# Moving the split weights' SBUF tensors 64 bytes down in a two-layer decoder trunk

## The reference

```python
h = rmsnorm(x, g_mix[0]);  x = x + gla_group(h, ...) @ w_out[0]
h = rmsnorm(x, g_ffn[0]);  x = x + (silu(h @ w_dense_gate) * (h @ w_dense_up)) @ w_dense_down
kv = rmsnorm(x, g_kv) @ w_kv                       # shared keys and values
h = rmsnorm(x, g_mix[1]);  x = x + diff_group(h, kv, ...) @ w_out[1]
h = rmsnorm(x, g_ffn[1]);  x = x + moe_swiglu(h, w_router, w_gate, w_up, w_down)   # top 2 of 8
out = rmsnorm(x, g_final)
```

## Time and profile before

| | us |
|---|---|
| median of 2 runs | 1590.91 |
| lowest and highest | 1589.26, 1592.56 |
| profiled execution | 1586.55 |
| its span, first to last instruction | 1584.8 |
| TensorE busy | 1499.1 (95% of the span) |
| VectorE busy | 1144.9 (72%) |
| ScalarE busy | 957.8 (60%) |

### The profile page before, as it was taken

The page is one execution under the profiler, slowest core; times in us unless marked ns, Lnnn a source line. Parts: engine busy times, 40 slices in busy tenths (PEclk is TensorE's granted clock), DMA queues, the critical chain, the costliest instruction groups (busy, mean ns, idle before and its releaser), DMA issues.

```text
span 1584.8 us, 19889 instructions
## 1 busy us (share of the span) xinstructions
PE 1499.1 (95%) x7534; PEld 1252.8 (79%) x7534; DVE 1144.9 (72%) x941; ACT 957.8 (60%) x868; POOL 7.9 (1%) x18
## 2 busy tenths in 40 slices
PE   4997899998978789999999999999999999999996
PEld 4995689998865668888887887887888888888885
DVE  3453454545557479879879878988887987987984
ACT  4553244334445377766767677767767677766773
POOL 1000000000000000000000000000000000000000
PEclk8995799999985899999999999999999999999998
DMA  9561154565512159989989999998997998998990
GB/s 295 184 206 53 54 169 164 187 209 185 165 54 80 53 195 384 387 298 375 387 319 347 385 334 335 384 376 287 394 376 288 384 380 289 385 385 285 380 384 29
DMA packets 201923, 428.34 MB, mean 270 GB/s; under 512 B 8848, under 2 KB 42672, under 8 KB 201872
## 3 DMA queue, kind: packets, MB, share of 16 engines
q1 hardware_dynamic: 200736, 424.18, 74.2%
q0 software_dynamic: 1136, 3.47, 0.9%
HBM read 426.57 MB, written 1.05 MB: 270 GB/s over the span
## 4 chain that ended last, share of the span: by engine, by line
PE 91%; DVE 5%; ACT 2%; DMA 1%; issue 1%; SPq 0%; DVEq 0%; ACTq 0%
PE ps L1130 27%; PE ps L1132 27%; PE ps L1131 27%; PE ps L1448 2%; PE ps L1426 2%; PE ps L1469 2%; DVE w_lo L682 1%; PE ps L1274 1%; DMA raw<-in_w_mem_kv_dram 1%; PE ps L1156 1%; PE ps L1249 1%; ACT w_hi L395 0%; PE ps L1327 0%; DVE small L739 0%; ACT sc L431 0%
## 5 line engine op out<-in xcount | busy, mean ns | idle before, releaser
L1063 DVE TENSOR_TENSOR e_wlo<-raw,e_whi 128x2048 fp32r<-128x2048 f32 x336 | 750.7, 2285 | 113.6 <-ACT e_whi L618 113.4
L618 ACT ACTIVATE e_whi<-raw 128x2048 fp32r<-128x2048 f32 x336 | 620.7, 1915 | 43.5 <-PE ps L1132 43.5
L1130 PE MATMUL ps<-e_whi,act_hi 128*128 128x512 f32 x1344 | 534.4, 398 | 2.9 <-DVE act_lo L1030 1.5
L1132 PE MATMUL ps<-e_wlo,act_hi 128*128 128x512 f32 x1344 | 523.9, 390 | 0.0
L1131 PE MATMUL ps<-e_whi,act_lo 128*128 128x512 f32 x1344 | 523.2, 389 | 0.0
L1130 PEld LDWEIGHTS ps<-e_whi,act_hi 128*128 128x128 f32 x1344 | 252.4, 188 | 57.5 <-issue 5.3
L1131 PEld LDWEIGHTS ps<-e_whi,act_lo 128*128 128x128 f32 x1344 | 252.6, 188 | 54.5 <-issue 3.8
L1132 PEld LDWEIGHTS ps<-e_wlo,act_hi 128*128 128x128 f32 x1344 | 252.3, 188 | 53.5
L682 DVE TENSOR_TENSOR w_lo<-raw,w_hi 128x2048 fp32r<-128x2048 f32 (+2 forms) x68 | 148.4, 2198 | 159.3 <-ACT w_hi L395 159.2
L395 ACT ACTIVATE w_hi<-raw 128x2048 fp32r<-128x2048 f32 (+2 forms) x68 | 124.1, 1839 | 105.7 <-PE ps L1132 89.7
L623 ACT ACTIVATE act_hi<-ps 128x512 fp32r<-128x512 f32 x56 | 33.5, 598 | 199.0 <-PE ps L1469 199.0
(11 more groups left out here) (200 smaller groups left out, 1116.9 us busy)
## 6 DMA issues: line engine op xcount, KB each, us to landing
raw<-in_w_exp_gate_dram SPq DMA_DIRECT2D x112, 1024.0 KB, 7.0
raw<-in_w_exp_up_dram SPq DMA_DIRECT2D x112, 1024.0 KB, 7.2
raw<-in_w_exp_down_dram SPq DMA_DIRECT2D x112, 1024.0 KB, 7.5
raw<-in_w_dense_gate_dram SPq DMA_DIRECT2D x11, 1024.0 KB, 5.2
raw<-in_w_dense_up_dram SPq DMA_DIRECT2D x11, 1024.0 KB, 5.4
raw<-in_w_dense_down_dram SPq DMA_DIRECT2D x11, 1024.0 KB, 5.7
raw<-in_w_out_dram SPq DMA_DIRECT2D x8, 1024.0 KB, 5.0
raw<-in_w_in_a_dram SPq DMA_DIRECT2D x7, 1024.0 KB, 6.6
```

Source lines behind the costliest of these rows:

```text
L618: nc.scalar.activation(e_whi[:, (s - NPRE) % E_SPLIT, :], raw[:, s % RAW, :], ACT.Copy)\
L1063: nc.vector.tensor_tensor(e_wlo[:, r, :], raw[:, s % RAW, :], e_whi[:, r, :].bitcast(F32), ALU.subtract).then_inc(lo_ready, 1)
L1130: nc.tensor.matmul(dst, l_hi, r_hi, start=start, stop=False)
L1132: return nc.tensor.matmul(dst, l_hi, r_lo, start=False, stop=stop)
```

## The change

The second padding becomes 264 numbers (1056 bytes), 64 bytes shorter:

```diff
-        sb("split_pad", [P, 280])
+        sb("split_pad", [P, 264])
```

## The result

| | before | after |
|---|---|---|
| median, us | 1590.91 (2 runs) | 1605.30 (2 runs: 1603.80, 1606.81) |
| profiled execution, us | 1586.55 | 1606.81 |
| its span, us | 1584.8 | 1605.0 |
| ratio, after to before | | 1.0106, 95% interval 1.0060 to 1.0152 |

The change makes the kernel about 1% slower, 9.5 to 24 us by the interval. The two spans differ by 20.2 us. A ratio of 1.0106 is inside what I called "within 2%", and the time is inside the range, but it is a real slowing and I had forecast none.

The account below looks back on a forecast made before the run. TensorE was taken as the bound, matmul count times distance; every term was 0, so 1586.55 + 0 = 1586.6 us profiled, 1590.9 as median (own range 1585 to 1600). The range that reached the rivals was 1550 to 1672.

Parts of the forecast that it names:

- within 2%: Whole kernel: the measured time lies within 2% of the time before, chance 0.55; slower 0.37, faster 0.08.
- What bounds the kernel: TensorE, never idle in an expert (125.00 of 125.00 us): time is the number of matmuls times what one costs.
- The count: Matmuls with an operand whose start moves: 5016 with weights moving, 1440 with weights stationary, together 6456.
- The step that failed: Price of a moving operand's new start: taken as 0 from 16-column operands at a 64-byte offset; ends 35 us faster, 920 slower.
- The term for stationary operands: Matmuls with weights stationary: 0 for the same reason as moving operands, up to 1440 x 4.2 = 6 us.
- The reading that the 13 ns are a wait for operands: Each matmul at full clock takes 13 ns beyond columns over clock, read as the array waiting for its operands.
- The bounds: Distance of matmuls in an expert: 219.7 ns if reads miss each other, 240 ns with one more piece per read.
- Rival 1: Moving reads fetched in 128-byte pieces need one more, 13.3 ns each: 67 us, 1658 us; chance 0.21, dearer form 0.13.
- Rival 2: Moving operands pay the 4.2 ns by phase seen for stationary ones: 21 us, 1612 us; chance 0.12.
- Rival 3: TensorE's moving and stationary reads, set 64 bytes apart, miss each other: wait falls to 6.3 ns, 1556 us; chance 0.11.
- Splits and their cover: VectorE and ScalarE splits: 0 change from 2285 and 1915 ns; each may grow 0.44 us before VectorE becomes the bound.
- The page rule: SBUF lines of 16 bytes: 64 bytes are four whole lines, accesses keep their place, so the sum is 0.

Follow-up runs that it names:

- w_only: The change for the stages before the experts alone, a 16-number padding putting the experts' tensors back; 1584.70 us, ratio 0.9980 to the kernel before the change.
- both_down: Split activations and split weights both 64 bytes lower than in the kernel before the change; 1588.33 us against 1588.67, ratio 0.9999.
- w128: The change with 128 bytes in place of 64, against the kernel before the change; ratio 1.0146, an expert 127.76 us.

## Why the prediction was right and wrong

- **What bounds the kernel** held. The effect in the experts is one distance times its count, TensorE stayed the bound, and nothing hid it: the experts' 24.1 us came through in full.
- **The count** held, but I multiplied it by a single price. By rows, 512-column matmuls with `act_hi` or `act_lo` stationary pay 6.6 ns (4560 of them; 6.0 as the mean over an expert), 256-column ones with 128 stationary columns gain 2 to 6 ns (1392 of them), those with 96 stationary columns 0.3 on the mean (117.9 to 117.6: one half of a slot loses nearly what the other gains), and the 264 of the dense down product pay nothing, as both their operands moved together.
- **The step that failed** is "Between ends so far apart the nearest row is the 64-byte offset that costs nothing ... I take 0". Those loads are 16 columns wide and 256 columns move over them, and their case says nothing of 512 columns moving over 128: such matmuls measured 6.6 ns with the same offset. The term for stationary operands, 0 "for the same reason", failed with it: they gained 2 to 6 ns. The sum should have been about +24 us in the experts and between -1.5 (by the distances) and -3 (by the medians of `w_only`) ahead of them.
- **The reading that the 13 ns are a wait for operands** fits all runs: at an unchanged 2.4 GHz (granted clock 1.00) the distance moved with the layout alone. That the wait is on the reading side was argued from it and is now likely; which of the reads waits is not shown.
- **The bounds** held: 233.3 is between 219.7 and 240. The range held the time, and was wide because I had no row between them; the forecast's own range, 1585 to 1600, did not hold it.
- **Rival 1** (one more piece per moving read) is refuted: 240 ns did not come, `both_down` has every moving read off its boundary for nothing, and 128 bytes, on the boundary, cost the same as 64.
- **Rival 2** (4.2 ns by phase, 1612 us) came nearest in microseconds, by accident: it charged the operand's own position, and `both_down` says that this costs nothing. What the earlier trace rows show is the same kind of effect, the position of the two reads to each other, as the halves that change places in `w128` show.
- **Rival 3** had the mechanism, the two reads' position to each other, with the wrong sign. I thought that both tensors at the same phase must be the bad place; for 512 columns it is the best of all that were tried, and only 256 columns over 128 stationary ones gained as this rival would have it. My argument against it ("with odd k the two are already 64 bytes apart and nothing changes") was the same mistake as the failed step.
- **Splits and their cover**: right, 2 and 5 ns.
- **The page rule.** The Trainium skill, in "Advanced Engine Details and Errata", section "SBUF Cachelines", and in "SBUF — State Buffer", section "Specifications (TRN2)", has lines of 16 bytes in SBUF, with full speed for accesses that hit the same line again. As I read it, that gave 0 for any multiple of 16 bytes. The rows disagree with this reading: 64 bytes lower gave 233.3 ns in place of 226.7. The measurement decides.

## What to carry to other kernels

Where TensorE is the bound, take the distance between matmul starts from the timeline and subtract the columns over the clock; if something is left, it may depend on where the stationary and the moving operand stand to each other in SBUF. Here, with 512 float32r columns moving, keep the difference of their addresses at a multiple of 256 bytes: every other offset that was tried cost some 2 to 7 ns in 226.7, and absolute alignment bought nothing. Other widths have another order of positions, so read the distance again for each. A row that shows no effect for a small operand is no evidence for a large one; if the trace has no such row, say so and give the unknown its full weight.

## What the runs showed of the hardware that I had not expected

- The distance of 512-column matmuls depends on the difference of two addresses with a period of 256 bytes: 226.7 ns at 0 and 256, 233 ns at 32, 64 and 128 bytes below, 229 to 230 at 64 above.
- With 256 columns moving and 128 stationary, in phase is not the best: 119.6 ns there, 113.3 to 118.0 with the weights 64 bytes lower, and the same slot with the same layout gave 113.3 in one trace and 118.0 in another. With 96 stationary columns in phase is the best again: 115.8 ns against 120.0 at 128 bytes.
- Moving `act_lo` alone by 128 bytes made two steps of three dear, 233 against 227 ns. Why the second pays is open, and so is which read waits for what; no experiment took the weight loads away from a matmul.
- 64 bytes lower had no effect on VectorE's and ScalarE's 2048-element instructions beyond 5 ns in 1915.
